# One-hot rows batched, the routing weights' exponentials moved, and identity transposes put into TensorE's three routing waits

## What is computed

```python
gl = (t @ w_group)                              # 4 groups
gi = argmax(gl); gw = softmax(gl)[gi]           # one group per token
el = einsum('nd,gde->nge', t, w_router)
esel = el[gi]                                   # 4 experts of that group
tv, ti = top_k(esel, 2); tw = softmax(tv) * gw  # two experts per token
for e in range(16):
    he = silu(t @ w_exp_gate[e]) * (t @ w_exp_up[e])
    out += dense_w[:, e:e+1] * (he @ w_exp_down[e])
```

## Time and profile before

| | |
|---|---|
| median of 3 runs | 938.31 us (937.93, 938.31, 939.45) |
| the profiled execution's own time | 938.0 us |
| its span, first to last instruction | 936.2 us |
| mean granted TensorE clock | 0.958 of full |
| PE busy | 836.3 us, 89% of the span |
| DVE busy | 468.7 us, 50% |
| ACT busy | 391.8 us, 42% |
| POOL busy | 189.7 us, 20% |
| DMA | 142.44 MB, mean 152 GB/s |

### The profile page before, as it was taken

How to read it: one execution, slowest core, us unless ns; L and a number is a source line. 1 busy time by engine, 2 the same in 40 slices (tenths; PEclk the granted TensorE clock), 3 DMA queues, 4 the chain that set the end, 5 groups by cost and what they waited for, 6 DMA issues and landing times.

```text
span 936.2 us, 13270 instructions
## 1 busy us (share of the span) xinstructions
PE 836.3 (89%) x5002; PEld 710.9 (76%) x5002; DVE 468.7 (50%) x778; ACT 391.8 (42%) x540; POOL 189.7 (20%) x131
## 2 busy tenths in 40 slices
PE   3999999999999999999999999999849899999910
PEld 3988878898788888878888888888737687778700
DVE  4511355454419632324231247533586888877537
ACT  4522244344432543333334113134425677668413
POOL 0001010000000001100100001300013487777543
PEclk9999999999999999999999999999859899999965
DMA  9215131322121313221220212893858899998675
GB/s 292 77 46 127 47 74 46 74 65 53 31 75 37 91 46 71 77 68 46 29 80 13 89 46 94 249 363 112 315 186 312 315 370 378 389 303 287 227 274 211
DMA packets 97261, 142.44 MB, mean 152 GB/s; under 512 B 4507, under 2 KB 75371, under 8 KB 97163
## 3 DMA queue, kind: packets, MB, share of 16 engines
q1 hardware_dynamic: 89276, 115.04, 36.6%
q0 software_dynamic: 7904, 26.44, 10.2%
q10 hardware_dynamic: 32, 0.26, 0.2%
HBM read 116.31 MB, written 25.43 MB: 151 GB/s over the span
## 4 chain that ended last, share of the span: by engine, by line
PE 74%; DVE 8%; DMA 6%; ACT 5%; issue 4%; SPq 2%; POOL 2%; ACTq 0%; POOLq 0%; DVEq 0%
PE main L828 20%; PE main L830 19%; PE main L829 19%; PE work L865 2%; PE work L895 2%; PE work L928 2%; PE work L912 2%; DMA expert_rows<-y_sb 1%; PE work L1076 1%; ACT prob_t L1200 1%; PE work L882 1%; DVE x L1867 1%; PE work L1031 1%; DMA raw<-in_w_in 1%; DMA e_raw<-in_w_exp_down 1%
## 5 line engine op out<-in xcount | busy, mean ns | idle before, releaser
L1440 DVE TENSOR_TENSOR w_lo<-raw,w_hi 128x2048 fp32r<-128x2048 f32 x30 | 68.7, 2290 | 259.8 <-ACT w_hi L1144 259.8
L828 PE MATMUL main<-ht_hi,w_hi 128*128 128x512 f32 (+1 forms) x576 | 196.9, 342 | 0.0
L829 PE MATMUL main<-ht_lo,w_hi 128*128 128x512 f32 (+1 forms) x576 | 193.9, 337 | 0.0
L830 PE MATMUL main<-ht_hi,w_lo 128*128 128x512 f32 (+1 forms) x576 | 193.8, 336 | 0.0
L828 PEld LDWEIGHTS main<-ht_hi,w_hi 128*128 128x128 f32 x576 | 109.2, 190 | 18.7 <-issue 4.7
L829 PEld LDWEIGHTS main<-ht_lo,w_hi 128*128 128x128 f32 x576 | 109.3, 190 | 11.6
L830 PEld LDWEIGHTS main<-ht_hi,w_lo 128*128 128x128 f32 x576 | 109.2, 190 | 11.7
L828 PE MATMUL main<-w_hi,ht_hi 128*128 128x256 f32 (+1 forms) x304 | 95.9, 315 | 3.4 <-DVE ht_lo L1457 3.4
L678 POOL DMA_DIRECT2D bias<-bias_vectors x16 | 12.4, 773 | 426.8 <-DVE nmx L1500 183.6
L830 PE MATMUL main<-w_hi,ht_lo 128*128 128x256 f32 (+1 forms) x304 | 93.5, 308 | 0.0
L829 PE MATMUL main<-w_lo,ht_hi 128*128 128x256 f32 (+1 forms) x304 | 93.5, 307 | 0.0
(11 more groups left out here) (262 smaller groups left out, 1518.9 us busy)
## 6 DMA issues: line engine op xcount, KB each, us to landing
e_raw<-in_w_exp_gate SPq DMA_DIRECT2D x16, 1024.0 KB, 8.2
e_raw<-in_w_exp_up SPq DMA_DIRECT2D x16, 1024.0 KB, 9.1
e_raw<-in_w_exp_down SPq DMA_DIRECT2D x16, 1024.0 KB, 8.5
raw<-in_w_in SPq DMA_DIRECT2D x28, 512.0 KB, 4.6
expert_rows<-y_sb SPq DMA_DIRECT2D x19, 512.0 KB, 8.0
raw<-in_w_in SPq DMA_DIRECT2D x9, 1024.0 KB, 5.2
expert_rows<-y_sb SPq DMA_DIRECT2D x1, 5632.0 KB, 22.4
raw<-in_w_out SPq DMA_DIRECT2D x4, 1024.0 KB, 6.0
```

The source lines that it names most:

```text
L828: pe.matmul(out, s_hi, m_hi, start=(first and i == 0), stop=False)
L829: pe.matmul(out, s_hi, m_lo, start=False, stop=False)
L830: last = pe.matmul(out, s_lo, m_hi, start=False, stop=(final and i == n - 1))
L1440: dve.tensor_tensor(w_lo[:, c % 2, :], raw[:, c % 2, :], w_hi[:, c % 2, :], ALU.subtract).then_inc(s_wlo, 1)
```

## The change

Three parts:

1. PE issues 28, 44 and 48 transposes of the identity matrix into a part of PSUM that nothing reads (`work[1][:, 512:640]`): 28 in front of the wait for `s_onehots`, 44 in front of the wait for `s_hot_slot`, 48 behind the 12 table matmuls, in front of the first `turn_rows`.
2. DVE's 24 one-hot instructions become six: per choice one `is_equal` over 6 x 32 elements, one over 6 x 128, and one multiplication over 6 x 32, which waits for the two before it. `s_hot_slot` is signalled once per choice, and PE's six matmuls of a choice wait for that.
3. `weight_differences` moves on DVE to the place between the one-hot rows and the wait for `s_table`. ACT's two exponentials move in front of `rows_hi(0, 0)`. DVE's `route_weights` moves into tile 0, between `rows_lo(0, 1)` and `hidden(0, 0)`.

```diff
+            def spin(n):
+                for _ in range(n):
+                    pe.transpose(work[1][:, 512:512 + P], ident[:, :], ident[:, :])
+
+            spin(28)
             pe.wait_ge(s_onehots, 1)
...
             pe.matmul(main[1][:, 0:96], mats[:, :], a96, start=True, stop=True).then_inc(s_rank, 1)
+            spin(44)
             for i in range(2 * NT):
                 k, t = divmod(i, NT)
-                pe.wait_ge(s_hot_slot, i + 1)
+                pe.wait_ge(s_hot_slot, k + 1)
...
             last.then_inc(s_table, 1)
+            spin(48)
...
             split_expert(0, 1, (0, 1, 2))
-            def route_weights():
-                act.wait_ge(s_diffs, 1)
...
+            act.wait_ge(s_diffs, 1)
+            act.activation(r24[:, 4, :, :], r24[:, 3, :, :], ACT.Exp).then_inc(s_rta, 1)
+            act.wait_ge(s_diffs, 2)
+            act.activation(r6[:, 5, :], r6[:, 4, :], ACT.Exp).then_inc(s_rta, 1)
...
             for j in range(3):
                 tile(0, j)
-                if j == 1:
-                    route_weights()
...
             for k in range(2):
-                for t in range(NT):
-                    dve.tensor_scalar(hot_tile[:, k, t, :], small[:, C_IOTA:C_IOTA + TILES_PAD], slots_f[:, 1, k, t:t + 1],
-                                      small[:, C_TOKEN + t:C_TOKEN + t + 1], ALU.is_equal, ALU.mult)
-                    dve.tensor_scalar(hot_slot[:, k, t, :], small[:, C_IOTA:C_IOTA + P], slots_f[:, 0, k, t:t + 1],
-                                      None, ALU.is_equal).then_inc(s_hot_slot, 1)
-
+                rt_on(dve.tensor_tensor(hot_tile[:, k, :, :], over(slots_f[:, 1, k, :], [P, NT, TILES_PAD], 2),
+                                        over(small[:, C_IOTA:C_IOTA + TILES_PAD], [P, NT, TILES_PAD], 1), ALU.is_equal))
+                rt_on(dve.tensor_tensor(hot_slot[:, k, :, :], over(slots_f[:, 0, k, :], [P, NT, P], 2),
+                                        over(small[:, C_IOTA:C_IOTA + P], [P, NT, P], 1), ALU.is_equal))
+                dve.wait_ge(s_rt, count[0])
+                dve.tensor_tensor(hot_tile[:, k, :, :], hot_tile[:, k, :, :],
+                                  over(small[:, C_TOKEN:C_TOKEN + NT], [P, NT, TILES_PAD], 2), ALU.mult).then_inc(s_hot_slot, 1)
+
+            weight_differences()
             dve.wait_ge(s_table, 1)
...
             def tile(r, j):
                 rows_lo(r, j + 1)
+                if not late(r, j, 1):
+                    route_weights()
                 hidden(r, j)
...
                 tile(0, j)
-                if j == 1:
-                    weight_differences()
-            route_weights()
```

More of the change, by code:

```diff
@@ L1351, in _ @@
             split_expert(0, 1, (0, 1, 2))
-            def route_weights():
-                act.wait_ge(s_diffs, 1)
-                act.activation(r24[:, 4, :, :], r24[:, 3, :, :], ACT.Exp).then_inc(s_rta, 1)
-                act.wait_ge(s_diffs, 2)
-                act.activation(r6[:, 5, :], r6[:, 4, :], ACT.Exp).then_inc(s_rta, 1)
+            act.wait_ge(s_diffs, 1)
+            act.activation(r24[:, 4, :, :], r24[:, 3, :, :], ACT.Exp).then_inc(s_rta, 1)
+            act.wait_ge(s_diffs, 2)
+            act.activation(r6[:, 5, :], r6[:, 4, :], ACT.Exp).then_inc(s_rta, 1)
             def rows_hi(r, j):
@@ L1739, in _, with weight_differences @@
             rt(dve.tensor_copy(slots_f[:, :, :, :], slots_u[:, 1:3, :, :]))
-            for k in range(2):
-                for t in range(NT):
-                    dve.tensor_scalar(hot_tile[:, k, t, :], small[:, C_IOTA:C_IOTA + TILES_PAD], slots_f[:, 1, k, t:t + 1],
-                                      small[:, C_TOKEN + t:C_TOKEN + t + 1], ALU.is_equal, ALU.mult)
-                    dve.tensor_scalar(hot_slot[:, k, t, :], small[:, C_IOTA:C_IOTA + P], slots_f[:, 0, k, t:t + 1],
-                                      None, ALU.is_equal).then_inc(s_hot_slot, 1)
+            def weight_differences():
+                rt(dve.tensor_reduce(value(0), gl, AX.X, ALU.max))
+                dve.tensor_tensor(four(3), gl, over(value(0), [P, NT, 4], 2), ALU.subtract).then_inc(s_diffs, 1)
+                rt(dve.tensor_reduce(value(2), four(5), AX.X, ALU.max))
+                rt(dve.scalar_tensor_tensor(four(7), best, LOWEST, four(5), ALU.mult, ALU.add))
+                rt(dve.tensor_reduce(value(6), four(7), AX.X, ALU.max))
+                dve.tensor_tensor(value(4), value(6), value(2), ALU.subtract).then_inc(s_diffs, 1)
+            for k in range(2):
+                rt_on(dve.tensor_tensor(hot_tile[:, k, :, :], over(slots_f[:, 1, k, :], [P, NT, TILES_PAD], 2),
[6 more added lines that the diff above has]
+            weight_differences()
             dve.wait_ge(s_table, 1)
@@ L1761, in _ @@
             dve.tensor_scalar(regs[:, 0, 0:1], regs[:, 0, 0:1], 2, None, ALU.subtract).then_inc(s_regs, 1)
[L1763 to L1770, removed]
             def route_weights():
```

## The result

The kernel after takes **930.79 us** (median of 4 runs, 930.09 to 931.50), the kernel before 938.78 beside it (4 runs, 937.93 to 939.45): a ratio of 0.9915 with the 95% interval 0.9898 to 0.9933. The forecast was 929.7, with a range of 927 to 941. One execution of the kernel without spins (4722.88 us) and two of the kernel before (2038.14 and 1054.90), all in that later set, were disturbed and are left out of every median. The time of the profiled execution is 931.3 us and its span 929.5; the mean granted clock rose from 0.958 to 0.975.

A forecast was written before the change was run, and what follows sets the result against it. The prediction took PE's waits in the routing and before tile 2, with the half-speed clock they cost, as the bound. Terms -2.9 + 0.5 - 6.2 = -8.6 from 938.0, plus 0.3 for the median, gave 929.7 us; range 927 to 941.

The forecast's parts named there:

- One-hot rows: Routing on DVE: batched rows take 3.2 us, so the table copy comes 1.1 or 0.6 us earlier.
- Weights' move: In front of `turn_hidden` of tile 2: the 3.2 us wait and the half-speed loss behind it go, -6.2 us.
- `route_weights` in tile 0: In front of `hidden(0, 0)`: its small third operation waits for POOL's first subtraction, costing 0.5 us (bounds 0 and 2).
- Transposes: PE, routing and tile 0: they count for the clock like matmuls, full speed from about 698.3; together -2.9 us.
- third rival: PE's routing: transposes do not count for the clock, all spins run at half speed; 940.3 us, slower; chance 0.30.
- that the gain lasts: DMAs, 694 to 750: 10.9 us of slack can be closed up by earlier loads, so the shift stays to the end.
- DMA rival: Half of the DMAs' slack stays open as loads wait for buffers: shift about 5.5 us, 932.5 us; chance 0.12.

The follow-up runs named there:

- that later set: Gathers from tile 5 on issued one subtraction earlier, with and without spins, beside the unchanged kernel after (931.16 us), it without spins (930.76) and the kernel before (937.55).

## Why the prediction was right, and where not

**One-hot rows: right.** From the first row to the last it took 3.15 us (684.22 to 687.37) against 3.2 forecast; the copy came 1.3 us earlier relative to the first row, a little more than the 0.6 to 1.1 forecast. Alone this is worth nothing in the median; in that kernel's profile what it saves is lost again behind a later wait for gathered rows.

**Weights' move: right, and the main part.** Forecast -6.2; tiles 2 to 5 show -6.9 after and -7.0 in the kernel with the weights alone. The wait went, and so did the half-speed stretch behind it. The excess of 0.7 is a term that the prediction let stand: the 0.72 us of issue in front of the loop went too. After, `turn_rows` (724.98) follows `turn_hidden` (724.76) without it.

**`route_weights` in tile 0: right.** It ends at 705.17 with the operation stretched to POOL's end, and `hidden` is 0.48 us behind the tanh; forecast 0.5.

**Transposes: right in mechanism, near in size.** They do lift the clock; the third spin, at half speed from 688.4 to 691.8, took 7.1 us, between the 5.3 and 10.2 of the two speeds. Tile 2 gained 3.4 us (2.7 in the second profile), where the terms gave 2.4 (-2.9 + 0.5). The prediction let the second `turn_rows` start as before; by the table's measure it starts 1.0 us early in the first profile and 0.1 in the second. The clock went from 0.50 to 1.00 with nothing but transposes running, in the kernel after and in that with the third spin alone, so the third rival falls. By the Trainium skill, page "TensorE: Matmul & The Clock Gate", Part 4 (PE-mode transpose), the full clock does not engage in transpose mode. These traces show otherwise, and they decide. But the prediction let the spins' saving stand in the sum, and at the end they are worth 0 to 0.9 us.

**The step that failed: "that the gain lasts".** The text took the slack of the DMAs from 694 to 750 for enough, and the gain after that as kept. The slack was closed up there (share 1.00 and 344 GB/s after, 0.88 and 306 before), but from tile 5 on PE ran ahead of the gathers and the loads, and 3.4 of 10.3 us went back, all of it by tile 13 (2.3 of 9.8 in the second profile). What the forecast lacked is POOL's part: a gather that is issued late, behind a subtraction and a copy. The DMA rival had the loss and its rough size (3.1 of 8.6 us), and one of its signs came: PE waited 1.60 us for gathered rows at 745.76 and again at 756.87, before 780. But it gave only one of the causes. The forecast still came out 1.1 us from the median since the local terms were too small by 1.7 and the loss was left out: two errors of opposite sign, so the agreement is partly luck. The third rival's 0.30 was too much, but no row before could tell. Its remark that the spins last 10 us longer at half speed is a slip: the prediction's own figures give 25.6 less 13.2, so 12.4, and no term hangs on it.

## What to carry to other kernels

When several savings fall in one stretch, follow the sum downstream: find the first engine or queue that paces that stretch next (here POOL's gathers, then the loads), and count a saving only up to its slack. Two limits close behind each other can hide each other, so an experiment that relieves one and shows no gain does not clear it. A small operation that another engine blocks is best moved to where nothing is queued behind it: that one move gave 5.3 us alone, of 6.4 to 8.0 for the whole change.

## What the runs showed of the hardware

- The granted clock went from 0.50 to 1.00 within an unbroken run of 128x128 fp32 transposes (at 691.8 in the kernel after, at 692.7 in that with the third spin alone), and two such runs stayed at full clock: 28 in 3.26 us and 44 in 4.97. It fell at 673.5 in the kernel before, while PE ran 20-column matmuls. In the kernel after it fell at 688.4, after 2.48 and 0.69 us of idle time and twelve 32-column matmuls; in its second profile at 685.3, in the idle time before those matmuls. So these two profiles do not single out the matmuls as the cause.
- The blocking between DVE and POOL goes both ways. DVE's 6-element operation was held 3.04 us, to the end of POOL's subtraction; two others beside the same subtraction, a reduce at 701.08 and a reciprocal at 701.28, were not (0.17 and 0.19 us). POOL's copy of one element a partition, otherwise mostly 0.2 us, took 2.24 at 785.12 in the kernel after and ended with a subtraction of DVE (787.32):

```profile
784.92 2.40 DVE L1621 TENSOR_TENSOR e_lo<-e_raw,e_hi 128x2048 fp32r<-128x2048 f32 x1 [1.43 <-ACT e_hi L1300]
```
